# Who issues the transposing DMAs of six FFNs: SyncE or ScalarE

## What is computed

```python
def swiglu(h, w_gate, w_up, w_down):
    return (jax.nn.silu(h @ w_gate) * (h @ w_up)) @ w_down

for l in range(DEPTH):
    h = rms_norm(x, ffn1_norm[l])
    x = x + 0.5 * swiglu(h, ffn1_w_gate[l], ffn1_w_up[l], ffn1_w_down[l])
    h = rms_norm(x, mix_norm[l])
    ...
    x = x + o @ w_out[l]
    h = rms_norm(x, ffn2_norm[l])
    x = x + 0.5 * swiglu(h, ffn2_w_gate[l], ffn2_w_up[l], ffn2_w_down[l])
```

## Time and profile before

| | |
|---|---|
| median of three runs | 1582.99 us (1582.68 to 1583.35) |
| the profiled execution | 1580.45 us, span 1578.7 us |
| mean granted clock of TensorE | 0.996 |
| PE busy | 1552.7 us, 98% |
| DVE busy | 1150.5 us, 73% |
| ACT busy | 893.7 us, 57% |
| POOL busy | 316.7 us, 20% |
| SP's queue (q1) | 291.82 MB, 59.6% of the 16 DMA engines |
| ACT's queue (q10) | 53.09 MB, 11.8% |

### The profile page before, as it was taken

How to read it: one execution, slowest core, us unless ns; L and a number is a source line. 1 busy time by engine, 2 the same in 40 slices (tenths; PEclk the granted TensorE clock), 3 DMA queues, 4 the chain that set the end, 5 groups by cost and what they waited for, 6 DMA issues and landing times.

```text
span 1578.7 us, 22063 instructions
## 1 busy us (share of the span) xinstructions
PE 1552.7 (98%) x7784; PEld 1293.3 (82%) x7784; DVE 1150.5 (73%) x1884; ACT 893.7 (57%) x1760; POOL 316.7 (20%) x371
## 2 busy tenths in 40 slices
PE   8999999999999999999999999999999999999998
PEld 6888888788888788888788888998788889878886
DVE  6788788778877687778878887767755578585563
ACT  6445477754436444477865444876544477674442
POOL 1233022032220223111123221001312110131210
PEclk9999999999999999999999999999999999999999
DMA  8999854289997999783359996642876556168670
GB/s 311 292 325 334 254 162 147 81 267 279 317 304 172 249 310 299 252 225 115 108 180 279 289 345 213 213 138 95 247 223 206 175 185 221 47 201 257 201 218 35
DMA packets 156045, 346.32 MB, mean 219 GB/s; under 512 B 73376, under 2 KB 74144, under 8 KB 155424
## 3 DMA queue, kind: packets, MB, share of 16 engines
q1 hardware_dynamic: 136944, 291.82, 59.6%
q10 hardware_dynamic: 18992, 53.09, 11.8%
HBM read 329.64 MB, written 1.06 MB: 209 GB/s over the span
## 4 chain that ended last, share of the span: by engine, by line
PE 89%; DVE 5%; issue 2%; ACT 2%; DMA 1%; POOL 1%; SPq 0%; POOLq 0%; DVEq 0%; ACTq 0%
PE PS L1034 26%; PE PS L1036 25%; PE PS L1035 25%; PE PS L1213 2%; PE PS L1234 2%; DVE Wl L1910 1%; PE PS L1276 1%; DVE QTl L1910 1%; PE PS L1374 1%; PE PS L1375 1%; PE PS L1376 1%; DMA raw<-in_ffn 1%; PE PS L1052 1%; PE PS L1256 1%; POOL st L2424 1%
## 5 line engine op out<-in xcount | busy, mean ns | idle before, releaser
L1910 DVE TENSOR_TENSOR Wl<-raw,Wh 128x1024 fp32r<-128x1024 f32 (+3 forms) x360 | 377.2, 1091 | 28.2 <-ACT Wh L1512 26.3
L1512 ACT ACTIVATE Wh<-raw 128x1024 fp32r<-128x1024 f32 (+3 forms) x360 | 308.9, 901 | 45.1 <-PE PS L1036 36.0
L1034 PE MATMUL PS<-Wh,Hh 128*128 128x512 f32 (+1 forms) x824 | 322.0, 391 | 2.6 <-DVE Hl L1970 2.2
L1036 PE MATMUL PS<-Wh,Hl 128*128 128x512 f32 (+1 forms) x824 | 318.8, 387 | 0.0
L1035 PE MATMUL PS<-Wl,Hh 128*128 128x512 f32 (+1 forms) x824 | 318.6, 387 | 0.0
L1910 DVE TENSOR_TENSOR QTl<-raw,QTh 128x1024 fp32r<-128x1024 f32 (+3 forms) x236 | 242.2, 1062 | 24.4 <-ACT QTh L1512 23.0
L1512 ACT ACTIVATE QTh<-raw 128x1024 fp32r<-128x1024 f32 (+3 forms) x236 | 202.1, 893 | 32.7 <-PE PS L1036 27.2
L1034 PE MATMUL PS<-QTh,Hh 128*128 128x512 f32 (+2 forms) x536 | 208.6, 389 | 0.2 <-DVE QTl L1910 0.2
L1036 PE MATMUL PS<-QTh,Hl 128*128 128x512 f32 (+2 forms) x536 | 206.4, 385 | 0.0
L1035 PE MATMUL PS<-QTl,Hh 128*128 128x512 f32 (+2 forms) x536 | 206.3, 385 | 0.0
L1597 ACT ACTIVATE WK<-PS,st 128x256 f32<-128x256 f32 x88 | 41.7, 473 | 283.4 <-PE PS L1036 253.0
(11 more groups left out here) (239 smaller groups left out, 2330.0 us busy)
## 6 DMA issues: line engine op xcount, KB each, us to landing
raw<-in_ffn SPq DMA_DIRECT2D x392, 512.0 KB, 5.6
BT<-in_ada ACTq DMA_DIRECT2D x96, 512.0 KB, 5.2
raw<-in_win SPq DMA_DIRECT2D x64, 512.0 KB, 5.0
raw<-in_wo SPq DMA_DIRECT2D x32, 512.0 KB, 5.5
raw<-in_win SPq DMA_DIRECT2D x8, 420.0 KB, 4.6
raw<-in_lat SPq DMA_DIRECT2D x6, 512.0 KB, 5.9
raw<-in_ffn SPq DMA_DIRECT2D x8, 256.0 KB, 5.5
BT<-in_nab SPq DMA_DIRECT2D x2, 1024.0 KB, 7.3
```

Of the source, the lines that this page charges most:

```text
L1034: e.matmul(out_, xh, wh, start=start, stop=False)
L1036: return e.matmul(out_, xl, wh, start=False, stop=stop)
L1512: ins = e.activation(high(p)[:, cc], raw[p % RAW][:, cc], ACT.Copy)
L1910: ins = e.tensor_tensor(low(p)[:, cc], raw[p % RAW][:, cc], high(p)[:, cc].bitcast(f32), ALU.subtract)
```

## The change

ACT issues the crossings. A function `with_crossings` puts cross(g,t) into ACT's list after the event that follows gu(g,t), as `with_packs` does for POOL; in the middle of an FFN that is right behind turn(g-1,t). At the start of stages 2, 3 and 5 ACT's list becomes gu(0,0), turn_x, cross(0,0), turn_x, gu(1,0), gu(0,1), cross(1,0), turn(0,0), cross(0,1), gu(1,1), and in stages 7 and 9 gu(0,0), gu(1,0), cross(0,0), turn_x, cross(1,0), turn_x, gu(0,1), turn(0,0), cross(0,1), gu(1,1). In stage 0 it is gu(0,0), the squares of the second tile, cross(0,0), gu(0,1), gu(1,0), cross(0,1), turn(0,0), cross(1,0), gu(1,1). Before a crossing of g over 0 ACT may round one more piece, if a slot is free. `weights_to` counts places without the crossings (`at`), so that the other entries are planned as before. SP's list has no crossings any more. POOL, DVE and PE are unchanged.

```diff
+def with_crossings(ev):
+
+    out, due = [], None
+    for e in ev:
+        out.append(e)
+        if due:
+            out.append(due)
+            due = None
+        if e[0] == "gu" and by_dma(e[1]):
+            due = ("cross", e[1], e[2], 0)
+    return out
...
     if kind == "f" and engine == "POOL":
         ev = with_packs(ev)
+    if kind == "f" and engine == "ACT":
+        ev = with_crossings(ev)
     return laid_end(s, engine, ev) if s in ENDS else ev
...
             if what in ("res", "xs"):
                 return 2 if g > 6 or g == 6 and what == "res" else 0
+            if what == "cross":
+                return 1 if g else 0
...
             for s in range(len(STAGES)):
+                at = -1
                 for i, ev in enumerate(order[s]):
                     top = n
+                    at += ev[0] != "cross"
...
-                        goal = (0, 12, 16, 16, 16, 18)[i] if s == 0 and i < 6 else n if laid else n + 2 * room(ev)
-                        while top < min(2 * NP, goal) and slot_free[top // 2] <= freed_before[s, i] + own:
+                        goal = (0, 12, 16, 16, 16, 18)[at] if s == 0 and at < 6 else n if laid else n + 2 * room(ev)
+                        while top < min(2 * NP, goal) and slot_free[top // 2] <= freed_before[s, at] + own:
...
-            crossings = {}
-            for s, (kind, k) in enumerate(STAGES):
-                for i, (what, g, t, _) in enumerate(DVE_WALK[s]):
-                    if what == "gu" and by_dma(g):
-                        crossings.setdefault(dve_weights[s, i] // 2 + RAW, []).append(cross_at((k, g, t)))
...
-                for m in crossings.get(p, ()):
-                    e.wait_ge(f_pack, m + 1)
-                    e.dma_start_transpose(crossed(m).rearrange("p (b q) -> p b q", b=4), packed(m)).then_inc(f_cross[m % 4], 16)
...
+            def cross(k, g, t):
+
+                m = cross_at((k, g, t))
+                e.wait_ge(f_pack, m + 1)
+                e.dma_start_transpose(crossed(m).rearrange("p (b q) -> p b q", b=4), packed(m)).then_inc(f_cross[m % 4], 16)
...
+                    elif what == "cross":
+                        cross(k, x, y)
```

## The result

The changed kernel took 1599.47 us (median of 4 runs, 1596.48 to 1600.72), the kernel before, beside it on the same chip, 1583.17 us (1582.68 to 1589.44): a ratio of 1.0094, 95% interval 1.0069 to 1.0119. The forecast was 1590.8 us, with 1584.5 to 1597.0 as its range. The side was right; the loss is 16.3 us, twice the 7.8 that I had summed, and outside the range.

A forecast was written before the change was run, and what follows sets the result against it. It took PE, busy 98% of the span, as the bound. Terms 0 + 5.8 + 1.8 + 0.2 + 0 gave +7.8 us on the 1582.99 us median, so 1590.8 us, range 1584.5 to 1597.

The forecast's parts named there:

- middle: Middle of the FFNs: 96 of the 108 crossings cost nothing, covered by idle time; without it up to 1.2 us each.
- three signs of being wrong: Transposing DMA takes ACT's queue much less than 1.2 us; first crossing lands within 4 us; PE waits in FFN middles.
- First Hl block: Start of stages 7 and 9: ACT waits for the pack and issues before turn_x, +1.9 us on PE's 1.09 us gap.
- rival (c): Stages 7 and 9: the forecast plus slow clock, 1.7 us more each, 1594 us; chance 0.30.
- term of 0.25 for the second crossing: Stages 7 and 9: its 1.20 us issue between the fourth and fifth Hh block costs about +0.25 us.
- down(0,1) of stages 7 and 9: Pieces delayed 2.3 us, less 1.1 us of DVE idle time and 0.45 us in hand: +0.75 us.
- Stages 2 and 5: Start of these stages: DVE begins its pieces later, so PE's 0.62 us gap grows by about 0.9 us each; bounds 0, 1.5.
- Stage 3: Start of the stage: same landing within 0.7 us, cross(0,1) costs DVE a quarter microsecond; +0.2 us, bounds -3.1 and +0.9.
- Stage 0: Start of the stage: first crossing lands at 30.5 instead of 30.6, PE's gap stays over 3 us; 0 us.
- rival (a): Crossing overtakes weight pieces on its own queue: -6 us in stage 0, -3.1 in stage 3, 1581.5 us; chance 0.12.

The follow-up runs named there:

- s1: Kernel before, with only the 84 crossings of the FFNs' middle issued by ScalarE, the first of them waiting for the previous landing: 1583.71 us, ratio 0.9996.
- s2: Changed kernel, with only the 24 crossings of g = 0 and 1 issued by ScalarE and all others left on SyncE's queue: 1601.03 us, ratio 1.0115.
- x2: Changed kernel with one weight piece of ScalarE ahead of the crossing of (0,1) in every FFN: 1591.43 us, ratio 1.0045.
- x3: Changed kernel with the first two in_ada loads of stages 2, 3 and 5 moved behind the silu of gu(1,0): 1594.44 us, ratio 1.0063.
- x6: Changed kernel with the rounding of (0,1) ahead of the fourth weight piece of gu(1,1): 1591.72 us, ratio 1.0047.
- b1: Kernel before with the first two in_ada loads of stages 2, 3 and 5 moved behind the silu of gu(1,0): 1581.17 us, ratio 0.9991.
- w1: Kernel before, with ScalarE waiting for each pack at the change's places but issuing nothing; SyncE issues all crossings: 1587.17 us, ratio 1.0023.
- x1: Changed kernel with the crossings of (0,0) and (1,0) behind both turn_x in stages 7 and 9: 1592.53 us, ratio 1.0055.
- x7_all_four: Changed kernel with four repairs together (later crossings, a weight piece ahead of cross(0,1), later in_ada loads, earlier rounding of (0,1)): 1576.08 us, ratio 0.9941.
- x7_again: Second timing of the changed kernel with all four repairs together, against the kernel before: 1575.66 us, ratio 0.9944.

## Why the forecast was wrong

**Bound, middle, what the change is: right.** The loss lies only where I placed it, the 84 later crossings are free (s1), the issue takes 1.21 us and lands in 4.1. I had counted 96 crossings as the middle; the other twelve were moved together with the starts, and no run tells them apart. None of the three signs of being wrong that I had named came.

**First Hl block: the gap right, the clock wrong in one stage, the second crossing too small in the other.** I had +1.9 on the gap of 1.09; it became 2.88, +1.8. In stage 7 the clock, which the forecast counted as kept and rival (c) as lost, cost 1.6 us more (3.4 - 1.8; the row of 1121.20 has 0.79 and 28 matmuls). In stage 9 it was kept (the row of 1418.00 has 1.00), and 0.6 us were lost all the same (2.4 - 1.8). That is the term of 0.25 for the second crossing:

```profile
1419.33 1.22 ACTq L1621 DMA_TRANSPOSE QF<-QF  x1
...
1419.95 0.40 PE L1046 MATMUL PS<-Wh,Hl 128*128 128x512 f32 x1
1420.39 0.50 PE L1044 MATMUL PS<-Wh,Hh 128*128 128x512 f32 x1
1420.59 0.91 ACT L1573 ACTIVATE Hh<-NW 128x128 fp32r<-128x128 f32 x4 [0.96 <-DVE NW L1975]
...
1420.93 0.90 DVE L1988 TENSOR_TENSOR Hl<-NW,Hh 128x128 fp32r<-128x128 f32 x4 [0.60 <-ACT Hh L1573]
```

ScalarE stands idle for 0.96 us behind the issue before its fifth Hh block, and PE's matmuls there start up to 0.44 us apart instead of 0.227. In s2, x2 and x3, wherever the clock is kept at this place, it costs 2.4 to 2.6 us as well.

**down(0,1) of stages 7 and 9: mis-sized by a misplaced idle time.** The step is "2.3 - 1.1 - 0.45 = +0.75". DVE before, in that stretch:

```profile
1119.40 5.14 DVE L1910 TENSOR_TENSOR Wl<-raw,Wh 128x1024 fp32r<-128x1024 f32 x4 [0.50 <-ACT Wh L1512]
...
1131.82 0.42 DVE L2005 TENSOR_TENSOR WK<-WK,PS 128x256 f32<-128x256 f32 x1 [1.13 <-ACT WK L1599]
```

The idle 1.13 us stand behind the tile of the earlier trace rows (1130.28), not ahead of it. From 1119.40 to the tile DVE has no break, so it can make nothing good. After, DVE starts its pieces at 1132.63, which is 2.4 us later once the 10.8 us by which everything is late there are taken off, and the tile (1143.51) is later by the same 2.4. Less the 0.45 us in hand that is 2.0, as measured at PE's first matmul there (1143.97 against 1131.13); 0.2 more come behind it. Stage 9 had the same and the slow clock on top, 1.7. Both repairs of this gap (x2, x6) took off 1.2 us each, the time of one piece.

**Stages 2 and 5: the gap 1.5 and 1.3 instead of 0.9, and a clock not thought of.** The pieces started where I had put them (337.38 us), but DVE 1.5 us later, and it is the bound there as in stage 7. Behind a gap of 2.10 us in stage 2 the clock was 0.79, 1.6 us more. The forecast weighed the clock in stages 7 and 9 alone.

**Stage 3: wrong in kind.** I took the number of packets ahead in the crossing's own queue for the cause and expected the same landing. It came after 10.3 us, not 9.1. PE lost 1.5 us at down(0,0) and behind it; then the gap at down(0,1) grew from 3.46 to 4.07, 0.6 us, and the clock of 0.62 behind it cost 1.2 us more than the 0.79 before. x3 and b1 show what makes the landing late: 1 MB of in_ada issued just before, which cost the crossing 4.3 us in its own queue and 3.3 us in the other. The loads stood there before the change too; what is new is the 1.0 us between the two. How the rest of the 3.4 us divides stays open. In the stretch between issue and first packet (514.4 to 518.3) the two queues moved, after:

```profile
q10 hardware_dynamic: 222, 0.84, 53.5%
q1 hardware_dynamic: 213, 0.77, 48.4%
```

That is close to the one-for-one of the earlier trace rows. It does not hold in every stretch: in the 5 us behind the issue in the kernel before (511.5 to 516.5) q1 moved 362 packets and q10 205. The Trainium skill ("DMA: Bandwidth & Descriptors", section "Issuing engines are not separate DMA queues") says that transfers of all issuing engines "interleave with each other, regardless of the engine that started them", and that a second issuer saves only issue time, "usually small relative to the DMA itself". The trace agrees with the first (222 packets against 213). Of the second it shows the other side: the issue saved on SyncE was idle time, and the same issue on ScalarE, 1.21 us with what it held up at 24 places, was the larger part of the loss, since the waits alone give a quarter (w1).

**Stage 0: right in the sum, by another route.** The first crossing landed 7.6 us after its issue, as before, and rival (a) is out. PE's gap of 5.0 us became three of 2.3, 1.5 and 1.8 us, where I had expected one of over 3. PE was 2.3 us ahead for a time, and at down(0,1) it was where it had been.

**The sum.** Of 19.4 us 11.4 are standstill (all of the 7.8 was forecast as such), 4 to 5 slow clock (forecast 0), and about 3 short delays within PE's busy time. The range fell short because it let (c) in at two places, at 1.7 us each, and its upper end had no room for a gap term that was too small at the same time.

## What to carry over

Moving a queue instruction onto a compute engine is free where the engine idles behind it, as 84 crossings were, and costs at its full length where it stands at a wait with nothing ahead of it to run beside. So judge each of its places apart, and put it behind work that someone waits for, not ahead. When a delay is to be absorbed, look on which side of the awaited instruction the idle time stands; and put a share of slow clock into the price of a new gap of PE: over all profiled runs the clock fell at a quarter of the gaps of 1.2 us and at 20 of the 35 of 1.8 to 3.0 us.

## What the runs showed of the hardware

The clock after a gap of middle length is no fixed outcome. Over the profiled runs of the changed kernel, s2, x1 and x3, PE had 17 gaps of 1.8 to 2.2 us in the FFNs; behind 8 of them the clock stayed up and behind 9 it fell, at about 1.6 us each. The ten gaps of 2.9 us at the first Hl blocks were no worse, over all profiled runs: the clock fell at five. Even the gap of 1.2 us in the mixers (L1223 in the waits above) did it in 7 of 28 cases, and there the price is 1.6 or 3.2 us. At the sixteen gaps of 1.09 us it never fell. The two profiled runs of the same kernel, x7_all_four and then x7_again, show both ends:

```profile
283.90:291.90 8.00, 8.00 (x25) 6.01 (x25) 5.47 (x14) 3.76 (x12) 0.00 (x0) 0.57 0.44 132
775.10:783.10 8.00, 7.96 (x24) 6.02 (x25) 5.54 (x14) 3.83 (x12) 0.00 (x0) 0.57 0.44 131
```

```profile
282.70:290.70 8.00, 8.00 (x43) 6.16 (x44) 6.17 (x16) 5.89 (x19) 0.00 (x0) 1.00 0.43 132
769.50:777.50 8.00, 7.96 (x36) 6.08 (x38) 5.55 (x14) 4.30 (x13) 0.00 (x0) 0.79 0.45 133
```

The first has a span of 1580.4 us, the second 1573.1; 3.2 and 1.6 of the 7.3 us between them lie behind these two gaps. That the scatter of the other times has the same source is likely, as the slower runs mostly show a lower mean clock, but only the profiled ones have a trace that shows it. What decides a single case was not tried.
